# Third block's gates and branches 512 columns wide with tokens in the partitions; two gates of each first-block layer placed between its branches

## The reference

```
for l in range(2):                                   # first block
    h = rmsnorm(x, g_mix[l]); proj = h @ w_in[l]     # gates, conv, three attentions' q, k, v
    ys = stack([conv, neighbourhood, dilated, window])          # 4 branches of 256
    branch = einsum('bsnc,ncd->bsnd', ys, w_branch[l])
    gates = sigmoid(gate_pre.reshape(b, s, 4, D) + gate_b[l])
    x = x + sum(gates * branch, axis=2) @ w_out[l]
    x = x + conv_ffn(rmsnorm(x, g_ffn[l]))           # 2816 wide
h = rmsnorm(x, norm_mix); proj = h @ w_in            # third block
branches = stack([y_ssd, y_lru, y_ret])              # 3 branches of 1024
branch_d = einsum('bskw,kwd->bskd', branches, w_branch)
gates = sigmoid(gate_pre.reshape(b, s, 3, D))
x = x + sum(gates * branch_d, axis=2) @ w_o
return rmsnorm(x + conv_ffn(rmsnorm(x, norm_ffn)), norm_final)   # 3072 wide
```

## Time and profile before

| | before |
|---|---|
| median of 3 runs | 1444.16 us (1442.37 to 7965.11) |
| the profiled execution | 1443.07 us, its span 1441.3 us |
| mean granted TensorE clock | 1.000 |
| TensorE busy | 1424.5 us, 99% of the span |
| GpSimd busy | 1184.1 us, 82% |
| ScalarE busy | 887.7 us, 62% |
| VectorE busy | 708.4 us, 49% |

### The profile page before, as it was taken

One profiled execution on the slowest core, in us unless ns is written; L12 is line 12 of the kernel. 1 busy time (PEld: TensorE's weight loads), 2 busy tenths in 40 slices (PEclk: granted clock), 3 DMA queues, 4 the chain that ended last, 5 costly groups with the idle time before them and its releaser, 6 DMA issues.

```text
span 1441.3 us, 28918 instructions
## 1 busy us (share of the span) xinstructions
PE 1424.5 (99%) x9384; PEld 1290.5 (90%) x9384; DVE 708.4 (49%) x1607; ACT 887.7 (62%) x1518; POOL 1184.1 (82%) x926
## 2 busy tenths in 40 slices
PE   9999999999999999999999999999999999999998
PEld 8899998888888899988888899999899999888887
DVE  4642445655555623356555555660663642544444
ACT  6565646766676655647666676866445544755555
POOL 6876687999969776787999979899576899799985
PEclk9999999999999999999999999999999999999999
DMA  7644454666657544555656566556444455565663
GB/s 252 190 158 146 136 170 152 201 196 191 188 162 219 164 152 140 160 176 155 207 192 189 189 212 193 158 168 203 123 143 131 149 188 178 166 203 186 191 190 98
DMA packets 80039, 250.91 MB, mean 174 GB/s; under 512 B 7633, under 2 KB 22481, under 8 KB 79569
## 3 DMA queue, kind: packets, MB, share of 16 engines
q1 hardware_dynamic: 79088, 244.81, 54.8%
q10 hardware_dynamic: 864, 4.92, 0.9%
HBM read 248.65 MB, written 1.05 MB: 173 GB/s over the span
## 4 chain that ended last, share of the span: by engine, by line
PE 95%; ACT 2%; DVE 2%; issue 0%; ACTq 0%; DVEq 0%
PE psum L1030 21%; PE psum L1031 20%; PE psum L1032 20%; PE psum L1062 16%; PE psum L1064 9%; PE psum L1149 1%; PE psum L1215 1%; PE psum L1168 1%; PE psum L1159 1%; PE psum L1137 1%; ACT w_hi L436 0%; PE psum L1216 0%; ACT arena L445 0%; PE psum L1176 0%; PE psum L1482 0%
## 5 line engine op out<-in xcount | busy, mean ns | idle before, releaser
L411 POOL TENSOR_TENSOR w_lo<-raw,w_hi 128x512 fp32r<-128x512 f32 x461 | 602.5, 1307 | 241.0 <-ACT w_hi L436 231.4
L412 POOL TENSOR_TENSOR w_lo<-raw,w_hi 128x512 fp32r<-128x512 f32 x461 | 609.2, 1322 | 0.0
L436 ACT ACTIVATE w_hi<-raw 128x1024 fp32r<-128x1024 f32 x461 | 485.8, 1055 | 179.4 <-PE psum L1064 84.4
L1030 PE MATMUL psum<-both,w_hi 128*128 128x256 f32 x1192 | 345.3, 290 | 0.0
L1032 PE MATMUL psum<-both,w_hi 128*128 128x256 f32 x1192 | 336.9, 283 | 0.0
L1031 PE MATMUL psum<-both,w_lo 128*128 128x256 f32 x1192 | 336.9, 283 | 0.0
L1062 PE MATMUL psum<-both,w_hi 128*128 128x512 f32 x1040 | 259.1, 391 | 0.0
L1030 PEld LDWEIGHTS psum<-both,w_hi 128*128 128x128 f32 x1192 | 228.0, 191 | 9.3 <-issue 8.5
L1031 PEld LDWEIGHTS psum<-both,w_lo 128*128 128x128 f32 x1192 | 228.2, 191 | 0.3
L1032 PEld LDWEIGHTS psum<-both,w_hi 128*128 128x128 f32 x1192 | 228.1, 191 | 0.0
L1062 PEld LDWEIGHTS psum<-both,w_hi 128*128 128x128 f32 x1040 | 190.7, 188 | 36.7
(11 more groups left out here) (297 smaller groups left out, 2202.6 us busy)
## 6 DMA issues: line engine op xcount, KB each, us to landing
raw<-in_units SPq DMA_DIRECT2D x461, 512.0 KB, 3.6
arena<-in_consts ACTq DMA_DIRECT2D x1, 2320.0 KB, 8.9
arena<-in_bias ACTq DMA_DIRECT2D x2, 1024.0 KB, 5.1
out<-arena SPq DMA_DIRECT2D x4, 256.0 KB, 2.7
arena<-in_consts SPq DMA_DIRECT2D x1, 768.0 KB, 7.1
pre<-in_x SPq DMA_DIRECT2D x2, 256.0 KB, 3.8
arena<-in_x SPq DMA_DIRECT2D x2, 256.0 KB, 4.6
prm<-in_params ACTq DMA_DIRECT2D x2, 153.5 KB, 3.1
```

The costliest lines, as they stand in the source:

```text
L411: pool.tensor_tensor(w_lo[s][:, 0:D // 2], raw[s][:, 0:D // 2], w_hi[s][:, 0:D // 2].bitcast(F32), ALU.subtract)
L412: pool.tensor_tensor(w_lo[s][:, D // 2:D], raw[s][:, D // 2:D], w_hi[s][:, D // 2:D].bitcast(F32), ALU.subtract)\
L436: act.activation(w_hi[s][:, :], raw[s][:, :], ACT.Copy).then_inc(hi_ready, d.inc(hi_ready))
L1030: pe.matmul(out, hi, r_hi, start=start, stop=False, **kw)
```

## The change

**Third block.** The gates and branches of all three passes are made by `column_part`: four units (512 outputs of one gate or branch) are loaded as four parts, each 2 chunks x 512 columns in pieces of 256 columns from four units (`load_columns`). TensorE holds 128 tokens stationary and streams 512 weight columns, 12 matmuls a unit, into a pair of slots, one per token half. Four gate units come first, then four branch units. The sigmoid is two ScalarE instructions of 128x512, multiply and add on VectorE also 128x512. `merged` lies by tokens and is turned back by two blocks of 8 transposes (`turn_merged`): behind the second part of the last branch, and behind the second output unit. ScalarE and VectorE make its parts straight from PSUM (`merged_highs`, `merged_lows`). The loops in this part are written out.

**First block, both layers.** The last two gate units leave their place behind the last `attend` and go behind the second and the third branch unit (`late_gate`), with their results in PSUM banks 0 and 1; the load order follows, and the slots that `mix` uses change places.

```diff
+LATE_GATES = 2
...
+GATED_AT = (41, 81, 97)
+AHEAD2 = 121
...
+        def merged_tokens(half, lo, n):
+            return a2("merged", half * D + lo, n)
+        def merged_turned(pair, c, lo=0, n=T):
+            return bank(4 + pair[c % 2], c // 2 % 2 * T + lo, n)
...
-                order = list(range(mixed)) + [mixed + k for k in BRANCH_ORDER]
+                branches = [mixed + k for k in BRANCH_ORDER]
+                order = list(range(mixed - 2)) + branches[:2] + [mixed - 2, branches[2], mixed - 1] + branches[3:]
...
+            def load_columns(first, k, s):
+                sp.wait_ge(hi_ready, d.next(hi_ready))
+                sp.wait_ge(lo_ready, d.next(lo_ready))
+                at, lo = third + first + k // 8 * 8 + k // 4 % 2, k % 4 * T
+                unit = t["units"][at:at + 7:2, :, lo:lo + T].rearrange("u p c -> p u c")
+                sp.dma_start(raw[s][:, :].rearrange("p (u c) -> p u c", u=4), unit).then_inc(raw_full[s], d.inc(raw_full[s]))
...
+                else:
+                    load_columns(first, u - first, (REAL + u) % RING)
...
+                    late = g - 4 * CH + LATE_GATES
                     act.wait_ge(unit_done, d.next(unit_done))
-                    act.activation(a1("gates", g * T, T), slot((UNITS_BEFORE + g) % RING), ACT.Tanh, scale=0.5,
+                    act.activation(a1("gates", g * T, T), slot((UNITS_BEFORE + g) % RING) if late < 0 else bank(late, 0, T), ACT.Tanh, scale=0.5,
...
                     if more:
                         exps(p + 1, 1)
-                    gate()
-                high()
-                gate()
+                        gate()
...
+                    act.activation(chunk(y_hi, CH + c), bank(7 - 2 * (c % 2), 0, T), ACT.Copy, scale=0.5)\
...
+                mixed_high(0)
                 high()
-                for c in range(CH):
-                    high(1 if c < 4 else 2)
+                d.skip(unit_done, 2)
+                gate()
+                high()
+                mixed_high(1)
+                high()
+                mixed_high(2)
+                d.skip(unit_done)
+                gate()
+                high(2)
+                mixed_high(3)
+                high()
+                for c in range(4, CH):
+                    high(2)
                     mixed_high(c)
...
+            def gate_rows(first=False):
+                act.wait_ge(unit_done, d.next(unit_done, 4))
+                if not first:
+                    act.wait_ge(branch_out, d.next(branch_out))
+                for half in range(2):
+                    act.activation(pre[:, half * 512:(half + 1) * 512], bank(4 + next_slot()), ACT.Sigmoid).then_inc(act_out, d.inc(act_out))
+            def branch_passes():
+                d.skip(unit_done, 4)
...
+            for g in range(2):
+                high(4)
+                gate_rows(first=g == 0)
+                high(4)
+                branch_passes()
...
+            gate_rows()
+            for y in range(4):
                 high()
...
-                    act.wait_ge(prod_ready, d.next(prod_ready))
...
+                head_high(y)
+            branch_passes()
+            for y in range(4):
                 high()
...
+                head_high(4 + y)
+            gate_rows()
+            high(4)
+            branch_passes()
+            def merged_highs(first):
+                pair = next_slot(), next_slot()
+                act.wait_ge(mt_ready, d.next(mt_ready))
+                for c in range(first, first + 4):
+                    if c - first >= 2:
+                        act.wait_ge(mlo_ready, d.next(mlo_ready))
+                    act.activation(chunk(y_hi, CH + c), merged_turned(pair, c), ACT.Copy).then_inc(mhi_ready, d.inc(mhi_ready))
...
+            for g in range(2):
+                high(4)
+                gate_rows()
+                high(2)
+                if g:
+                    branch_passes()
+                    merged_highs(0)
+                    high(2)
+                else:
+                    high(2)
+                    branch_passes()
+            high(2)
+            merged_highs(4)
+            high(CH - 3)
...
-                    fill()
+                    if more:
+                        fill()
...
-                fill()
...
+                def late_gate(b):
+                    s = unit()
+                    for c in range(CH):
+                        last = mm3(bank(b, 0, T), blocks_of(w_hi[s], c), blocks_of(w_lo[s], c), chunk(h_hi, c), chunk(h_lo, c), c == 0, c == CH - 1)
...
                 for c in range(LAG + 1):
                     branch_unit(act_free if c < 2 else slot_free)
+                    if c in (1, 2):
+                        late_gate(c - 1)
+                pe.wait_ge(act_free, d.next(act_free, LATE_GATES))
...
+            def column_part(hi, lo, part, pair):
+                s = unit()
+                w = [w[s].rearrange("p (u c x) -> p c u x", u=4, c=2) for w in (w_hi, w_lo)]
+                for half in range(2):
+                    for c in range(2):
+                        at = 2 * part + c, half * P, P
+                        last = mm3(bank(4 + pair[half]).rearrange("p (u x) -> p u x", u=4), hi(*at), lo(*at), w[0][:, c], w[1][:, c],
+                                   part == 0 and c == 0, part == 3 and c == 1)
+                last.then_inc(unit_done, d.inc(unit_done))
+            def gate_columns(free=slot_free, between=lambda part: None):
+                pe.wait_ge(free, d.next(free, 2))
+                pair = next_slot(), next_slot()
+                for part in range(4):
+                    column_part(lambda *at: part_of(h_hi, *at), lambda *at: part_of(h_lo, *at), part, pair)
...
+                pe.wait_ge(free, d.next(free, 2))
+                pair = next_slot(), next_slot()
+                for part in range(4):
+                    column_part(lambda c, lo, n: y_hi[:, (first + c) * T + lo:(first + c) * T + lo + n],
+                                lambda c, lo, n: y_lo[:, (first + c) * T + lo:(first + c) * T + lo + n], part, pair)
+                    between(part)
...
-            gated_branch(act_free)
+            gate_columns(act_free)
+            pe.wait_ge(ylo2_ready, d.next(ylo2_ready, CH))
+            branch_columns(0, act_free)
+            gate_columns()
+            branch_columns(0)
...
+            def turn_merged(first):
+                pe.wait_ge(slot_free, d.next(slot_free, 2))
+                pe.wait_ge(merged_ready, d.next(merged_ready))
+                pair = next_slot(), next_slot()
+                for c in range(first, first + 4):
+                    for half in range(2):
+                        last = pe.transpose(merged_turned(pair, c, half * P, P), merged_tokens(half, c * P, P), ident)
+                last.then_inc(mt_ready, d.inc(mt_ready))
+            gate_columns(act_free, beside_gates)
             pe.wait_ge(ylo2_ready, d.next(ylo2_ready, 4))
-            linear_unit(y1_hi, y1_lo, free=act_free)
...
+            branch_columns(CH, act_free, beside_branch)
+            gate_columns()
+            branch_columns(CH)
+            gate_columns()
+            pe.wait_ge(ylo2_ready, d.next(ylo2_ready, CH))
+            branch_columns(0)
+            gate_columns()
+            branch_columns(0, between=lambda part: turn_merged(0) if part == 1 else None)
             pe.wait_ge(rn_ready, d.next(rn_ready, RET_H))
...
-                pe.wait_ge(ylo2_ready, d.next(ylo2_ready))
+                pe.wait_ge(mlo_ready, d.next(mlo_ready))
                 token_rows(s, y1_hi, y1_lo, c, 0, first=(c == 0))
                 token_rows(s, y1_hi, y1_lo, c, 1, first=(c == 0)).then_inc(unit_done, d.inc(unit_done))
-            last_two_turning(y1_hi, y1_lo, CH - 2, ylo2_ready)
+                if c == 1:
+                    turn_merged(4)
...
-                    one, two = bank(4 + 2 * b), bank(5 + 2 * b)
...
+            def free_gates():
+                dve.wait_ge(act_out, d.next(act_out, 2))
+                next_slot(), next_slot()
+                dve.sem_inc(slot_free, d.inc(slot_free, 2))
+            def gated_rows(g, pair, first=False, final=False):
+                d.skip(unit_done, 4)
+                dve.wait_ge(unit_done, d.next(unit_done, 4))
+                for half in range(2):
+                    here, done = bank(4 + pair[half]), branch_out if half else vec
+                    out = merged_tokens(half, g * 512, 512) if first else here
+                    dve.tensor_tensor(out, here, pre[:, half * 512:(half + 1) * 512], ALU.mult).then_inc(done, d.inc(done))
+                if not first:
+                    dve.wait_ge(vec, d.made(vec))
+                    dve.wait_ge(branch_out, d.made(branch_out))
+                    for half in range(2):
+                        part, done = merged_tokens(half, g * 512, 512), merged_ready if half and final else vec
```

(41 more changed lines are left out.)

130 lines of the change are left out of this document (45 added, 85 removed).

## The result

The changed kernel takes 1434.92 us (median of 4 runs, 1434.66 to 1435.09) against 1443.34 for the kernel before; the ratio is 0.9944, 95% interval 0.9932 to 0.9957. The 1443.34 is the median of four runs, one of which took 7965.11 us; the ratio leaves that one out (the other three: 1442.37, 1442.51 and 1444.16). The profiled execution took 1435.09 us, its span is 1433.3, the granted clock 1.000.

The account below looks back on a forecast made before the run. TensorE was taken as the bound, with matmuls running 99% of the span. From the profiled execution, 1443.07 - 7.7 (width) - 1.8 (waits) + 1.8 (turns) - 1.2 (layers) = 1434.2 us; own range 1431.5 to 1437, full range 1431.5 to 1439.

Parts of the forecast that it names:

- Width: Third block's 48 gate and branch units: 512-column matmuls take each from 2.88 to 2.72 us, saving 7.7 us.
- Waits removed in the third block: Waits before each stage's first branch unit, covered by four gate units instead of one: 0.70 + 1.11 = 1.8 us saved.
- Turns: Third block: two blocks of 8 transposes turn the merged sum back, adding 2 x 0.88 = 1.8 us.
- the cover of 2.6 us: Third block, second turn: two output units of 5.4 us cover VectorE's 2.8 us of multiplies and adds, leaving 2.6 us.
- Head products: Retention stage: VectorE's second four end about 3 us before their release is needed; costs 0 to 2 us, taken as 0.
- Layers: First two layers: moving two gates removes 1.8 us of mix waits, adds 1.2 us; net 0.6 us a layer.
- The new wait: First two layers: first branch waits about 1.1 us for the last y_lo, with 0.1 for the matmul after it.
- the least distance behind the late gates: First two layers: GpSimd's end stays at least about 1.2 us ahead of TensorE's start.
- Rival 1: Third block: weights can't follow; with half the units at the old 2.88 us, 3.8 us lost, 1438; chance 0.13.
- Rival 2: Third block: GpSimd sets the pace everywhere, 3.28 us a unit for all 48 units, 1461 us; chance 0.03.
- Rival 3: Third block: a 512-column matmul costs two of 256, 0.240 us, so width gives nothing, 1441.9 us; chance 0.04.
- Rival 4: First two layers lose: cover taken from y_lo costs more than 1.8 us each, say 2.5, so 1436.8; chance 0.04.

Follow-up runs that it names:

- e4: The changed kernel with each 512-column matmul of the third block's 48 gate and branch units issued as two of 256 columns; 1442.31 us.
- e2: The kernel before with the layers' edits alone: last two gates of each layer behind the second and third branch unit; 1443.00 us, ratio 0.9993.
- e8: The kernel before with VectorE's 16 later adds of the third block reading the product from PSUM instead of SBUF; 1442.50 us, ratio 0.9997.
- e5: The changed kernel with each of the 2 x 8 transposes of the merged sum done twice into the same place; 1436.20 us, ratio 0.9954.
- e6: The changed kernel with the second turn straight behind the last branch unit instead of behind the second output unit; 1438.79 us, ratio 0.9973.
- e3: The changed kernel with one late gate instead of two in each layer, behind the second branch unit; 1432.68 us, ratio 0.9924.
- e7: The changed kernel with products of gate and branch written to SBUF, so eight 128x512 adds take both inputs from SBUF; 1434.98 us, ratio 0.9949.

## Why the prediction was right, point by point

- **Width, 7.7 us.** Units of 2.72 us in both stages, and e4 gives 7.4 us back when the matmuls are halved; the first six units of the second stage, between whose matmuls retention's own stand, gave 0.76 us where six times 0.16 is 0.96. The step that took the earlier trace rows as the price of the same form in another place held to 0.01 us a unit.
- **Waits removed in the third block, 0.70 and 1.11 us.** Both are gone. The first is there in every trace of a kernel with the old order (0.51 to 0.60 over); the second is real in the earlier trace rows but comes from the add's collision with GpSimd (e2, e8), absent in e2. As a term against the profiled execution it was right; how much of it a median holds stays open.
- **Turns, 1.8 us.** 0.79 + 0.09 each, as in the earlier trace rows; e5 and e6 show that they are fully paid and that the cover of 2.6 us was 2.4.
- **Head products.** The end of the second four was placed 3 us ahead of its release and called the thinnest cover. Their last low part ends at 1146.34 and the slots released behind it are needed at 1154.10, 7.8 us. The cost of 0 was right, the cover of the slots was larger, and the thinnest cover lay elsewhere (below the list): four products with their low parts were set at 12 us where the trace has 4.3 + 5.8.
- **Layers, net 0.6 us each.** 0.59 and 0.58. The new wait was put at 1.1 + 0.1 and is 1.16 + 0.07; the least distance behind the late gates was put at 1.2 and is 1.38. Both terms were right, and yet the sum missed what e3 shows: the forecast noted that with one gate between "the mix is done", but did not ask whether the second gate was still needed.
- **Rival 1, the weights** (0.13): no unit of the stages waited, least distance 1.16 us. The column loads landed after 3.7 us, nearly as whole units do (3.6), not after the 4.4 of the earlier trace rows, so the load's form costs nothing here. **Rival 2** did not come either, but there was less room than the forecast thought (below the list). **Rival 3** (width gives nothing) is refuted by e4, and with it the 1.5 us that rival 3 works out by the rule for a lone matmul in the Trainium skill (TensorE: Matmul & The Clock Gate, Back-to-back issue gap): measured are 7.4. **Rival 4**: the layers gained.
- **Sum.** 1434.2 against 1435.09 in the profiled execution. Of the 0.9 between them, 0.6 lies ahead of unit 8, where first loads land, and is not the change's; 0.2 at the first six units of the second stage; and 0.1 around the output product. Behind unit 8 the change gives 8.6 us where the terms say 8.9.

The forecast looked for the thinnest cover at the slots behind the head products. The traces have it at the weights of the same place. ScalarE and GpSimd of the changed kernel, timeline:

```profile
1137.58 0.42 ACT L972 ACTIVATE y_hi<-arena 128x256 fp32r<-128x256 f32 x1 [3.92 <-DVE arena L2339]
```

```profile
1139.02 1.30 POOL L439 TENSOR_TENSOR w_lo<-raw,w_hi 128x512 fp32r<-128x512 f32 x1 [1.76 <-ACT w_hi L464]
```

ScalarE waits 3.92 us for a head product that VectorE has yet to make. The rounding of the next unit to w_hi stands behind that y_hi in its program, and GpSimd waits 1.76 us for the rounding. With another 1.76 us of this kind ahead of 1126.21, 1.17 us behind the sigmoids, and halves of 1.47 us beside VectorE's low parts, GpSimd's end on a unit, which is 6.1 us ahead of TensorE at unit 355 (1126.90), is only 1.16 us ahead at unit 363 (1148.66). The kernel before had 2.69 us there at the least. That this cost nothing follows from the lead of 6 us, which the forecast had not worked out; in this part it was lucky.

## What to carry to other kernels

When a bound engine streams short instructions, price a wider form by start-to-start times of the nearest stretch that already uses it, and subtract what the changed layout costs to turn back: here 48 x 0.16 against 2 x 0.88 us. When work is moved to fill a wait, move one piece and follow both ends before moving a second: one gate removed both waits for the mix, the second one only uncovered the wait that it had been covering. And before a wait in one trace is counted as gained, look at whether the instruction ahead of it has an unusual duration; an add of 1.59 us among others of 0.42 to 0.91 was a collision, and a kernel with the same code at that place did not have it.

## Not expected of the hardware

- VectorE's add of two SBUF tiles and GpSimd's subtraction, started within 0.01 us of each other, took 1.59 and 1.30 us in one kernel's trace and 0.42 and 1.57 in another's; such an add from PSUM took 0.42 us all 16 times (e8).
- Eight such adds of 128x512 in e7 took 0.71 to 1.41 us and left the time alone, but took 0.9 us from the distance at which the weights run ahead.
- The part ahead of unit 8 differs by up to 1.6 us between profiles of kernels that are equal there (-0.4 to +1.2 us against the kernel before). With effects of 1 us, the starts of the same unit in two traces tell more than the medians of 5 runs.
